# Experts' weights in runs of 8 KB per partition, with a strided moving operand in the gate and up matmuls

## The reference, cut to what matters

```
g = xb @ w_gate[e]                      # (rows, 1024) @ (1024, 512)
u = xb @ w_up[e]                        # (rows, 1024) @ (1024, 512)
y = (silu(g) * u) @ w_down[e]           # (rows, 512) @ (512, 1024)
out[token] += weight * y[row of the token]
```

## Time and profile before

| | |
|---|---|
| median of 3 runs | 1971.59 us (1971.11 to 1974.7) |
| profiled execution, first to last instruction (span) | 1969.2 us |
| TensorE matmul busy, whole span | 1726.2 us (88%) |
| stretch of the experts' loads at full rate | about 317 us to 812 us |
| bytes moved in that stretch | 194.13 MB |

### The profile page before, as it was taken

How to read it: one execution, slowest core, us unless ns; L and a number is a source line. 1 busy time by engine, 2 the same in 40 slices (tenths; PEclk the granted TensorE clock), 3 DMA queues, 4 the chain that set the end, 5 groups by cost and what they waited for, 6 DMA issues and landing times.

```text
span 1969.2 us, 33581 instructions
## 1 busy us (share of the span) xinstructions
PE 1726.2 (88%) x14289; PEld 1453.8 (74%) x14295; DVE 902.2 (46%) x1395; ACT 643.4 (33%) x859; POOL 43.5 (2%) x53
## 2 busy tenths in 40 slices
PE   6997988877777777699999969999899997889998
PEld 6986887544444344389998769998799986479998
DVE  3775454110111011265557755555755557635554
ACT  4543542101110011243344144334433344334332
POOL 2000000000000000000000400000000000000000
PEclk9998989988998889899999989999999998589999
DMA  9543336999999999945554024555255552024550
GB/s 298 173 150 118 111 112 229 394 394 394 395 394 394 394 394 394 362 155 189 188 180 149 18 86 149 188 179 187 86 184 181 190 184 93 22 65 150 192 182 32
DMA packets 252586, 410.01 MB, mean 208 GB/s; under 512 B 6887, under 2 KB 157566, under 8 KB 252524
## 3 DMA queue, kind: packets, MB, share of 16 engines
q1 hardware_dynamic: 250544, 404.55, 59.0%
q0 software_dynamic: 1744, 4.53, 0.8%
q10 hardware_dynamic: 236, 0.06, 0.0%
HBM read 408.06 MB, written 1.05 MB: 208 GB/s over the span
## 4 chain that ended last, share of the span: by engine, by line
PE 64%; DMA 19%; DVE 7%; SPq 4%; ACT 3%; issue 1%; POOL 0%; DVEq 0%; ACTq 0%; POOLq 0%
PE bank L517 18%; PE bank L518 17%; PE bank L519 17%; DMA odd_expert<-in_w_up_dram 13%; DMA raw<-in_w_up_dram 5%; SPq L404 4%; PE bank L934 2%; PE bank L600 2%; PE bank L626 2%; DVE prob L1725 2%; PE bank L529 2%; DVE wlo L1469 1%; PE bank L773 1%; ACT xn L1102 1%; DMA raw<-in_w_in_dram 1%
## 5 line engine op out<-in xcount | busy, mean ns | idle before, releaser
L1945 DVE TENSOR_TENSOR wlo<-raw,whi 128x2048 fp32r<-128x2048 f32 x120 | 275.1, 2292 | 274.5 <-ACT whi L1352 274.5
L1352 ACT ACTIVATE whi<-raw 128x2048 fp32r<-128x2048 f32 x120 | 229.7, 1914 | 279.2 <-PE bank L519 279.2
L517 PE MATMUL bank<-x1hi,whi 128*128 128x256 f32 x976 | 279.4, 286 | 2.2 <-DVE x1lo L1501 2.2
L518 PE MATMUL bank<-x1hi,wlo 128*128 128x256 f32 x976 | 276.2, 283 | 0.0
L519 PE MATMUL bank<-x1lo,whi 128*128 128x256 f32 x976 | 276.1, 283 | 0.0
L517 PE MATMUL bank<-x0hi,whi 128*128 128x256 f32 x880 | 249.5, 284 | 1.0 <-DVE x0lo L1501 1.0
L518 PE MATMUL bank<-x0hi,wlo 128*128 128x256 f32 x880 | 249.0, 283 | 0.0
L519 PE MATMUL bank<-x0lo,whi 128*128 128x256 f32 x880 | 249.0, 283 | 0.0
L1469 DVE TENSOR_TENSOR wlo<-raw,whi 128x2048 fp32r<-128x2048 f32 x71 | 162.2, 2290 | 73.2 <-ACT whi L1080 72.7
L517 PEld LDWEIGHTS bank<-x1hi,whi 128*128 128x128 f32 x976 | 187.3, 192 | 5.8 <-issue 4.8
L518 PEld LDWEIGHTS bank<-x1hi,wlo 128*128 128x128 f32 x976 | 187.3, 192 | 1.7 <-issue 0.7
(11 more groups left out here) (290 smaller groups left out, 2546.5 us busy)
## 6 DMA issues: line engine op xcount, KB each, us to landing
raw<-in_ffn_w_gate_dram SPq DMA_DIRECT2D x44, 1024.0 KB, 5.3
raw<-in_ffn_w_up_dram SPq DMA_DIRECT2D x44, 1024.0 KB, 5.3
raw<-in_ffn_w_down_dram SPq DMA_DIRECT2D x44, 1024.0 KB, 4.9
raw<-in_w_gate_dram SPq DMA_DIRECT2D x32, 1024.0 KB, 16.0
raw<-in_w_up_dram SPq DMA_DIRECT2D x32, 1024.0 KB, 14.8
raw<-in_w_down_dram SPq DMA_DIRECT2D x32, 1024.0 KB, 14.0
odd_expert<-in_w_gate_dram SPq DMA_DIRECT2D x32, 1024.0 KB, 15.3
odd_expert<-in_w_up_dram SPq DMA_DIRECT2D x32, 1024.0 KB, 14.5
```

The costliest lines, as they stand in the source:

```text
L517: pe.matmul(dst, a_hi, b_hi, start=first, stop=False, skip_group_check=True)
L518: pe.matmul(dst, a_lo, b_hi, start=False, stop=False, skip_group_check=True)
L1352: act.activation(whi[:, c0_ % SPLIT, :], raw[:, c0_ % RAW, :], ACT.Copy).then_inc(hi_ready, 1)
L1945: dve.tensor_tensor(wlo[:, c0_ % SPLIT, :], raw[:, c0_ % RAW, :], whi[:, c0_ % SPLIT, :].bitcast(F32), ALU.subtract).then_inc(lo_ready, 1)
```

## The change

Row r of an expert's weights goes to another place. With `"e (p k) n -> p e k n"` partition p gets the rows 8 p to 8 p + 7 of w_gate and w_up (four in each slot) and the rows 4 p to 4 p + 3 of w_down (two in each slot). These rows are neighbours in memory, so a slot is 128 runs of 8 KB.

The matmuls follow. The gathered activations must have feature 8 p + k on partition p of tile k, so the gather's stationary operand takes every eighth feature (`xn[:, tt, k:D:KT]`). The hidden row index must come out as 4 p + j, so column tile j of gate and up takes every fourth column of the weights (`w_k[:, k % 4, j:D_EXPERT:4]`). The down matmul, all waits and the order of the issues are as before.

```diff
             def load_expert(x, parity, slot, sem_):
                 if slot < 4:
-                    a = ins["w_gate" if slot < 2 else "w_up"][0].rearrange("e (k p) n -> p e k n", p=P)
+                    a = ins["w_gate" if slot < 2 else "w_up"][0].rearrange("e (p k) n -> p e k n", p=P)
                     src = a[:, bass.ds(x, 1), 4 * (slot % 2):4 * (slot % 2) + 4, :]
                     dst = expert_slot(parity, slot).rearrange("p (o k n) -> p o k n", o=1, k=4)
                 else:
-                    a = ins["w_down"][0].rearrange("e (k p) n -> p e k n", p=P)
+                    a = ins["w_down"][0].rearrange("e (p k) n -> p e k n", p=P)
...
-                        mm = pe.matmul(dst[:, (k % 4) * width:(k % 4) * width + width], xn[:, tt, k * P:k * P + P],
+                        mm = pe.matmul(dst[:, (k % 4) * width:(k % 4) * width + width], xn[:, tt, k:D:KT],
                                        src[:, tt, 0:width], start=tt == 0, stop=tt == TT - 1, skip_group_check=True)
...
                             mm = pe.matmul(ps[4][32 * j:32 * j + 32, which * P:which * P + P], x_of(k),
-                                           w_k[:, k % 4, j * P:j * P + P], start=k == 0, stop=k == KT - 1,
+                                           w_k[:, k % 4, j:D_EXPERT:4], start=k == 0, stop=k == KT - 1,
                                            skip_group_check=True)
...
-                                    pe.matmul(ps[5][:, k * SLOTS:k * SLOTS + SLOTS], xn[:, tt, k * P:k * P + P],
+                                    pe.matmul(ps[5][:, k * SLOTS:k * SLOTS + SLOTS], xn[:, tt, k:D:KT],
                                               sel[:, tt, 0:SLOTS], start=tt == 0, stop=tt == TT - 1, skip_group_check=True)
```

## The result

The changed kernel takes 1991.65 us (median of 4 runs, 1990.69 to 1994.15), the kernel before 1973.14 us beside it. The ratio is 1.0094 with a 95% interval of 1.0078 to 1.0109: slower by 0.9%, 18.5 us, where 32 us were forecast to be won. The profiled span is 1992.2 us against 1969.2 us.

What follows compares the result with a forecast made beforehand. Weight loads were taken to bound the experts' stage (495 us at 392 GB/s). Faster loads gave -32.1 us, both strided operands 0: 1971.6 - 32.1 = 1939.5 us, own range 1929 to 1957, 8 in 10 from 1929 to 2000.

Steps and rivals of the forecast that it cites:

- The bound before: Experts' stage, 317 to 812 us: loads set the pace at 392 GB/s; TensorE waits 85.9 us and needs 409 of 495.
- The loads: Expert weight loads: 8 KB packets reach 422 GB/s, continuing 387 and 410; gate and up -27.8 us, down -4.3, together -32.1.
- Rival 1: Expert weight loads: the rate doesn't rise with longer rows; 1965 to 1981 us, chance 0.12.
- The strided moving operand: Gate and up matmuls reading at a step of four: no visible loss; a factor up to 1.36 stays hidden.
- the middle bound: Gate and up matmuls: twice as long per element at full clock, 1.94 us a slot, 247.5 us against 149.9, +98 us.
- The strided stationary operand: Gather matmuls reading at a step of eight: taken as 0; doubled, at most +32 us, bare only in the last gather.
- the 54 us of spare: Experts' stage: TensorE's margin under the faster loads, 409 us needed against 463 us of loads.
- Rival 2: Experts' stage: TensorE becomes the bound, gate and up matmuls twice as long per element; 1964 to 2016 us, middle 1984, chance 0.20.
- the wide range: Whole kernel: the range of 8 in 10, 1929 to 2000 us, leaving out Rival 3.
- Rival 3: Gate and up matmuls: four column tiles read the same 16-byte places in turn, +348 us of TensorE; about 2213 us, chance 0.13.
- The signs named: Changed profile, if the read penalty exists: 32 records take 1.9 us at full clock, no DMA waits, DMA share below 1.

Runs made afterwards that it cites:

- the first three runs: Against the kernel before: gate/up 8 KB runs with strided gather, 1948.91 us; w_down 8 KB runs with moving step four, 1969.06 us; all steps two, 1947.96 us.
- first experiment: Against the kernel before: gate and up weights in 8 KB runs and the gather at a step of eight, w_down and moving operand unchanged; 1948.91 us.

## Why the prediction was wrong, step by step

**The bound before** was right. The waits of 86 us are real spare time: the half with the strided moving operand used nearly all of it and lost nothing.

**The loads** were right. 8 KB packets run at 422 to 424 GB/s for a predicted 422, and the mixtures follow the same three rates: from 340 to 780 us the first three runs moved 418, 398 and 413 GB/s, where 387, 410 and 422 for their rows of 2, 4 and 8 KB give 418, 398 and 414. The stage with all loads long and almost no read penalty is 33.8 us shorter for a predicted 32.1. The rule of an overhead of 3 beats for each packet, in the Trainium skill (DMA: Bandwidth & Descriptors, Why small descriptors are slow), would have given 414.7 GB/s and 24 us, the estimate in the prediction; the measurement decides for the line through the rows. Rival 1 is out.

**The strided moving operand** is the step that failed. The text took "no visible loss, since the nearest rows of matmul reads, those of float32r, are at twice the needed rate". The factor is 2.04 (7.56 / 3.70) at full clock, and +90.7 us over the stretch, of the +98 that stood as the middle bound. That is a factor of 1.6 on the 149.9 us of the stretch, where the prediction put the point at which the win is gone at 1.57. The argument counted elements where the price goes by lines. The float32r row reads 256 contiguous elements in 120 ns, a quarter of a line each, that is 1.88 ns per line: if the price of a line holds for it, that row had no reserve at all. (That the float32r matmul itself is held by the read wasn't tested; the clock could hold it just as well.) The step of four asks for a line every 0.9 ns and gets one every 1.85.

**The strided stationary operand** failed as well: taken at 0, it is the full doubling, +31.3 us in the stretch and 3.9 us more in the two bare calls at the end (4.07 + 3.84 us against 2.05 + 1.95). The remark that even then the 54 us of spare would hide it is true alone (first experiment) and false beside the other step. Both prices were weighed against the same spare time one at a time. Together they are 122 us against 54.

**The rivals.** Rival 2 came in, with both its terms: 409 + 98 - 20 + 32 = 519 us against 495 is +24, and the stage grew by 17.1. Its "middle 1984" is 1971.6 + 12, with neither the clock nor the gather in it; with all its terms it would have been 1996, for a measured 1991.65. The forecast's own range, 1929 to 1957, misses the result; only the 0.20 given to this rival carried the wide range up to 2000. The rule of the Trainium skill (SBUF — State Buffer, The DMA port swizzle) agrees with the runs: full bandwidth needs at least two hits in a 16-byte line. The step of two has them and pays 6%; the steps of three, four and eight have fewer on average and pay 56% to 108%. Rival 3 is out: the four streams don't get into each other's way, neighbours (7.56 us) or not (7.54 us).

**The signs named** at the end of the prediction read as rival 2 word for word: 1.9 us a slot at full clock, no waits on DMA, a DMA share of 0.96.

## What to carry to other kernels

Longer runs in memory raise the rate of a stage that loads hold (387, 410, 422 GB/s at 2, 4 and 8 KB), but the new order has to be paid for where the data is read. Count the 16-byte lines that a float32 matmul's operand touches, moving and stationary, at about 1.9 ns each, and put the permutation where it stays at two elements a line, or where it is done once. When several edits draw on the same spare time of an engine, add their prices before comparing them with it: here each half won and the whole lost.

## What the runs showed of the hardware that I had not expected

The price of a line doesn't follow TensorE's clock: a strided slot took 2.04 us at a granted clock of 0.50 (1.2 GHz) and 2.03 us at 1.00 (2.4 GHz). The four column tiles read independently, yet one slow stream sets the time of its set (7.67 us with one strided tile, 7.56 with four). VectorE pays for a step of eight in one of its inputs too: 2.27 us in place of 1.41 for its two multiplications by a scalar, 3.92 us in place of 2.36 for the two products with the gain.
